# State products of a recursion cut in halves, an addition put behind a negation, an affine step on another engine, and identity products joined

## What is computed

```python
def step(s, inp):                       # the recurrent mixer, per head
    r_t, w_t, k_t, v_t, kk_t, b_t = inp
    sa = jnp.einsum('bhvk,bhk->bhv', s, kk_t)
    s = s * w_t[:, :, None, :] - sa[..., None] * b_t[:, :, None, :] + v_t[..., None] * k_t[:, :, None, :]
    y = jnp.einsum('bhvk,bhk->bhv', s, r_t)
    return s, y
...
z = layer_norm(z, conv_ln_w, conv_ln_b)  # the convolution half
z = z * jax.nn.sigmoid(z)
...
x = x + jnp.concatenate([y_a, y_b], axis=-1) @ w_out
x = x + moe_ffn(h2)                      # top 4 of 32 experts, w_gate, w_up, w_down
```

## Time and profile before

| | us |
|---|---|
| median of 3 runs | 1165.84 (1164.99 to 1166.95) |
| the profiled execution | 1165.45 |
| its span, first to last instruction | 1163.6 |
| PE busy | 1122.2 (96%) |
| DVE busy | 529.1 (45%) |
| ACT busy | 212.3 (18%) |
| bytes moved | 430.00 MB, mean 370 GB/s |

### The profile page before, as it was taken

One profiled execution on the slowest core, in us unless ns is written; L12 is line 12 of the kernel. 1 busy time (PEld: TensorE's weight loads), 2 busy tenths in 40 slices (PEclk: granted clock), 3 DMA queues, 4 the chain that ended last, 5 costly groups with the idle time before them and its releaser, 6 DMA issues.

```text
span 1163.6 us, 16613 instructions
## 1 busy us (share of the span) xinstructions
PE 1122.2 (96%) x6608; PEld 480.4 (41%) x6608; DVE 529.1 (45%) x1123; ACT 212.3 (18%) x433; POOL 34.1 (3%) x47
## 2 busy tenths in 40 slices
PE   9999999999999999999999999999999999999997
PEld 7666786643333333333333333333333333333332
DVE  6999965337333333333333333333333333333333
ACT  3265642221111111111111111111111111110012
POOL 0002412000000000000000000000000000000000
PEclk9999999999999999999999999999999999999999
DMA  9724006999999999999999999999999999999995
GB/s 247 214 86 179 20 16 175 429 392 415 417 427 427 429 428 430 427 429 427 430 429 427 430 427 430 428 429 427 430 427 429 430 426 430 429 429 427 429 421 204
DMA packets 58587, 430.00 MB, mean 370 GB/s; under 512 B 16670, under 2 KB 29390, under 8 KB 34220
## 3 DMA queue, kind: packets, MB, share of 16 engines
q1 hardware_dynamic: 58288, 428.84, 89.7%
q10 hardware_dynamic: 260, 0.61, 0.2%
HBM read 424.92 MB, written 4.48 MB: 369 GB/s over the span
## 4 chain that ended last, share of the span: by engine, by line
PE 53%; DMA 29%; DVE 4%; issue 1%; ACT 1%; DVEq 0%; ACTq 0%
PE bank L2166 35%; DMA ring<-in_w_up_dram 26%; PE bank L2133 5%; DMA arena<-in_w_up_dram 3%; PE bank L2140 2%; PE bank L2086 2%; PE bank L1734 2%; DVE arena L2536 1%; DVE arena L2560 1%; PE bank L1312 1%; PE bank L1271 1%; PE bank L2174 1%; PE bank L2192 1%; PE bank L1320 0%; PE bank L278 0%
## 5 line engine op out<-in xcount | busy, mean ns | idle before, releaser
L2166 PE MATMUL bank<-arena 128*64 128x512 f32 x1540 | 344.2, 594 | 11.4 <-DMA arena<-in_w_up_dram 11.2
L2166 PE MATMUL bank<-ring,arena 128*64 128x512 f32 x1532 | 342.2, 594 | 11.8 <-DMA ring<-in_w_up_dram 11.0
L2166 PEld LDWEIGHTS bank<-arena 128*64 128x64 f32 x1540 | 108.0, 136 | 225.8 <-issue 197.9
L2166 PEld LDWEIGHTS bank<-ring,arena 128*64 128x64 f32 x1532 | 108.0, 137 | 225.2 <-issue 198.0
L2560 DVE TENSOR_TENSOR arena<-arena,bank 128x512 f32<-128x512 f32 x180 | 110.0, 680 | 0.0
L2549 DVE SCALAR_TENSOR_TENSOR arena<-bank,arena 128x512 f32<-128x512 f32 x31 | 23.3, 751 | 182.0 <-ACT arena L1928 182.0
L2536 DVE TENSOR_SCALAR arena<-bank 128x512 f32<-128x512 f32 x31 | 21.4, 692 | 179.9 <-PE bank L2174 179.9
L610 PE MATMUL bank<-arena,ring 128*128 128x336 f32 x352 | 102.5, 447 | 0.3 <-DVE arena L751 0.3
L2133 PE MATMUL bank<-arena 128*64 128x512 f32 x372 | 86.7, 599 | 4.3 <-DVE arena L2560 0.6
L1904 ACT COPY arena<-bank 128x512 f32<-128x512 f32 x31 | 18.2, 587 | 354.3 <-PE bank L2133 354.3
L610 PEld LDWEIGHTS bank<-arena,ring 128*128 128x128 f32 x352 | 65.8, 189 | 34.2 <-issue 2.9
(11 more groups left out here) (387 smaller groups left out, 785.5 us busy)
## 6 DMA issues: line engine op xcount, KB each, us to landing
ring<-in_w_gate_dram SPq DMA_DIRECT2D x32, 2048.0 KB, 29.8
arena<-in_w_up_dram SPq DMA_DIRECT2D x32, 2048.0 KB, 32.8
arena<-in_w_gate_dram SPq DMA_DIRECT2D x32, 2048.0 KB, 29.9
arena<-in_w_down_dram SPq DMA_DIRECT2D x31, 2048.0 KB, 35.4
ring<-in_w_down_dram SPq DMA_DIRECT2D x31, 2048.0 KB, 35.4
ring<-in_w_up_dram SPq DMA_DIRECT2D x29, 2048.0 KB, 32.9
ring<-in_w_in_dram SPq DMA_DIRECT2D x11, 1024.0 KB, 8.4
ring<-in_w_up_dram SPq DMA_DIRECT2D x11, 512.0 KB, 7.3
```

The lines of the kernel that those rows point to most:

```text
L2166: mm = M.matmul(bank[64 * hb:64 * hb + 64, b, :], tokens(cc), rows[:, 512 * hb:512 * hb + 512], start=(cc == 0), stop=(w3 == 2 and cc == K ...
```

## The change

Four edits, all in the scan:
1. `state(j)` is cut into `state(j, 0)` and `state(j, 1)`. The half for r = 0 stays at the end of step j; the half for r = 1 runs in step j + 1, behind W and the identity product and ahead of U. `st_done` is raised by the second half.
2. On DVE the addition to `sout` stands behind the negation of U instead of ahead of it.
3. The affine step of `zT` moves from DVE (one quarter ahead of the loop, one in each of three steps) to ACT: four activations with scale and bias, in place, between the first and second `take_v`.
4. The eight identity products of a step become one product with the whole 128 x 128 identity over 256 columns; the eight products with `identc` in step 0 become two over 256 columns each.

```diff
@@ scan_act
             take_v(0)
+            for j in range(4):
+                nc.scalar.activation(zT[:, j, :], zT[:, j, :], ACT.Identity, bias=vecA[:, V_CLB + j:V_CLB + j + 1],
+                                     scale=vecA[:, V_CLW + j:V_CLW + j + 1]).then_inc(S["z_scaled"], 1)
             take_v(1)
@@ scan_pe
-            def state(j):
...
-                for r in range(2):
-                    for i in range(2):
-                        at = 64 * i + 32 * r
-                        mm = M.matmul(bank[side(r), 6 + i, 0:256], VU[2][at:at + 32, i, 1, j, :],
-                                      KBxx[at:at + 32, j, i], start=True, stop=True)
-                mm.then_inc(S["st_done"], 1)
+            def state(j, r):
+
+                if r == 0:
+                    if j == 0:
+                        pe.wait_ge(S["e_ready"], 4)
+                        pe.wait_ge(S["un5_ready"], 2)
+                    else:
+                        pe.wait_ge(S["sout_ready"], j)
+                for i in range(2):
+                    at = 64 * i + 32 * r
+                    mm = M.matmul(bank[side(r), 6 + i, 0:256], VU[2][at:at + 32, i, 1, j, :],
+                                  KBxx[at:at + 32, j, i], start=True, stop=True)
+                if r == 1:
+                    mm.then_inc(S["st_done"], 1)
@@ the loop
-                    each(4, identity, kept_state, 64, C, True, False)
+                    M.matmul(bank[:, 4, 0:256], ident, Zc.rearrange("p j k -> p (j k)"), start=True, stop=False)
+                    state(c - 1, 1)
@@
                 if c == 0:
-                    each(7, lambda i, j: identc, lambda i, j: szb[:, i, j, 0, :], 64, C, True, False)
+                    for i in range(2):
+                        M.matmul(bank1(7)[side(i)], identc, szb[:, i, :, 0, :], start=True, stop=False)
@@
                 if c < 4:
-                    state(c)
+                    state(c, 0)
@@ scan_dve
-            z_affine(0)
             level(5, 0)
             level(5, 1)
@@ the loop
+                dve.wait_ge(S["u_done"], c + 1)
+                negated(c // 2, c % 2, 2).then_inc(S["un_ready"], 1)
+                if c:
                     dve.wait_ge(S["old_read"], c)
                     dve.wait_ge(S["st_done"], c)
                     kept = sout[:, c - 1, :].rearrange("p (s i k) -> p i s k", s=4, i=2)
                     V.tensor_tensor(kept, bank[:, 6:8, 0:256].rearrange("p i (s k) -> p i s k", s=4), kept, ALU.add)\
                         .then_inc(S["sout_ready"], 1)
-                dve.wait_ge(S["u_done"], c + 1)
-                negated(c // 2, c % 2, 2).then_inc(S["un_ready"], 1)
@@
-                if c < 3:
-                    z_affine(c + 1)
```

More of the change, by code:

```diff
@@ L988, in build @@
         names = ["v_turned", "vtok_ready", "hat_ready",
-                 "last_turned", "last_copied", "z_scaled", "z_sig", "zT_ready",
+                 "last_turned", "last_copied", "z_scaled", "zT_ready",
                  "kb_turned", "kbtok_ready", "sc_done", "sc_read", "blk_done",
@@ L1081, in scan_act @@
                 nc.scalar.activation(zsg[:, j, :], zT[:, j, :], ACT.Sigmoid, bias=vecA[:, V_CLB + j:V_CLB + j + 1],
-                                     scale=vecA[:, V_CLW + j:V_CLW + j + 1]).then_inc(S["z_sig"], 1)
+                                     scale=vecA[:, V_CLW + j:V_CLW + j + 1])
             def take_v(p):
@@ L1331, in rows @@
                 return v[64 * i:64 * i + n]
-            def identity(i, j):
-                return ident[side(i), side(i)]
             def chunk(c):
@@ L1553, in level @@
                                 b2(clow[:, l - 4, :], 8), ALU.mult).then_inc(S["e_ready"], 1)
[L1555 to L1558, removed]
             dve.wait_ge(S["kb_turned"], 6)
```

## The result

The changed kernel takes 1166.84 us (median of 18 runs, 1165.62 to 1169.19), the kernel before 1164.92 us in as many runs beside it (1163.07 to 1166.95). The ratio is 1.0019, with a 95% interval of 1.0013 to 1.0026: the change makes the kernel **2.2 us slower**, 1.5 to 3.0 (the two medians are 1.9 us apart). The forecast was +2.0 us, or +0.17%, and 1167.8 us.

What follows compares the result with a forecast made beforehand. PE's own order bounds the scan, the expert weight stream the back. Steps sum to 0.46 + 0.50 + 0.50 + 0.57 - 0.03 = +2.00 us; 1165.45 + 2.00 + 0.39 gives 1167.8 us, range 1164.5 to 1169.4.

Steps and rivals of the forecast that it cites:

- The bound: Behind the scan, the expert weight stream bounds; a PE shift reaches the end one to one, at least 2.8 us if earlier.
- rival (c): Behind the scan: PE's shift doesn't reach the end, as the stream is set by its start at 196.94; 1165.8 us, chance 0.06.
- A half costs what the whole costs: State products in the scan: a half takes 0.56 us (0.53 to 0.59) against 0.59 for the whole.
- Rival (a): In the scan: halves cost half, shapes nothing extra; -1.05 us, 1164.8 us (best case 1163.9), chance 0.13 with its best case.
- the second rival: What the prediction said a reading by instruction counts alone would give; second in its list stands Rival (b).
- the joined product: Between W and the second half of state: 0.62 us, 0.43 of work and 0.19 for leaving the shape.
- Rival (b): In the scan: each extra change of shape costs 0.25 us, 12 extra blocks, +3.2 us, 1169.1 us, chance 0.18.
- The sum: W to U 1.54 us in place of 1.01; +0.50 in steps 2 and 3, +0.57 in step 4, +2.00 in all.
- the change behind W: Change of tile shape between W and the whole-array identity product: 0.13 us.
- The stall of step 1: W's instructions stall 0.24 us in step 1; if that stays, W to U is 1.78 against 1.29, +0.46 us.
- Cost 0: DVE's addition moved behind the negation: at most 0.03 us gain per step, taken as 0, and no cost.
- The cover of 0.18: On DVE: the moved addition would end about 172.45, 0.18 us ahead of the next evacuation at 172.63.

Runs made afterwards that it cites:

- SP late: The kernel before with one more wait of SP ahead of the first expert weights, which start 5.0 us later: ratio 0.9999 of before (0.9990 to 1.0008).
- PE late: The kernel before with ten extra whole-array products of 336 columns into an unused bank in step 4: ratio 1.0042 of before (1.0028 to 1.0056), 4.9 us longer.

## Why the prediction was right, and where it wasn't

- **The bound.** Right: SP late cost nothing that shows (0.9999), which with the 2.2 us also ends rival (c); PE late and PE earlier (no state products) both moved the end in the size of their shift, within their intervals. One reading was loose: the waits for weights are summed from 230 us on the earlier trace rows, but the first of them comes at 610 us. Up to there PE carries a shift along by itself; only behind it does the place of the stream, which by the windows is set by about 294 us, take over.
- **A half costs what the whole costs.** Right, a little more than said: 0.58 for either half, where 0.56 was taken, and 0.59 for the whole. Rival (a), halves at half the price, is dead: W starts 0.58 after the half, not 0.30. (It is this one, and not the second rival, that a reading by instruction counts gives.)
- **Changes of shape.** W's group took 0.39 with its change where 0.36 was summed, the joined product 0.63 where 0.62 was. Rival (b), 0.25 for each change, didn't come (its sum, 1165.84 + 3.2, is 1169.0 and not 1169.1).
- **The sum.** W to U is 1.60, forecast 1.54; per step +0.58, forecast +0.50. In step 4 +0.59, forecast +0.57. The whole loop is +2.28 without the stall, forecast +2.00. The mis-sized terms are the half (0.02 too small, twice), the change behind W (0.03) and the joined product (0.01).
- **The stall of step 1.** The sum took 0.24 for something that may belong to the step. It doesn't: it was absent in the second trace of before and in both of after, and present in the trace with the late PE and in the one with the products unjoined.
- **Luck in the number.** Trace against trace the loop grew by 25.59 - 23.58 = 2.01, which looks like the forecast to the hundredth. But the terms were 0.28 too small together, and the 0.27 of the stall, which happened to be in this trace of before and not in that of after, hides it. The 1167.8 lies 1.0 above the median measured, mostly because the kernel before had a median of 1164.92 in the runs beside it and not the 1165.84 of its first three.
- **The second edit.** "Cost 0" holds for the change as a whole and for this edit alone, but the reasoning missed its worth: with the halves it saves 0.32 us in each of steps 1 and 2 (4.48 to 4.16), since the halves make the addition late. (Between these two kernels the affine step moved too; the chain shows the addition as what was waited for.) The cover of 0.18 behind it came out as 0.14.
- **The fourth edit.** Beside the halves it costs 0.18 per step in steps 1 to 3 (4.16 to 4.34). The forecast's terms hold 0.13 + 0.62 for it where the eight products took 0.46 and a change behind them, which the prediction puts at 0.16, so 0.13; measured it is 1.60 against 1.42. Alone it gains about 0.2 in the loop by sharing the shape of the projection, which the forecast didn't see.
- **The third edit.** No effect, as said: ACT waited 1.02 behind it where 0.9 was forecast.
- **First weights.** Forecast at 197, seen at 198.42, and at 199.58 in the second trace of the unchanged kernel, so the change isn't needed for it. It was of no consequence, as SP late shows.
- **Behind the loop.** The prediction looked only for transfers in the chain there. That DVE, with POOL beside it, could make PE later by 0.6 us was not in the sum; the last section tells it.

## What to carry to other kernels

Products that sit side by side in different parts of the array took the time of one here (0.59 us for four, 0.58 for two): halving their number halved nothing, and the second half paid in full in its new place. Count the changes of tile shape (0.10 to 0.20 us each in these traces) beside the instructions, and put a product beside one of its own shape. Before work is moved to another step, look for what is queued behind it on the other engines. If two traces are to be compared for where a shift of a few microseconds went, take a second trace of the same kernel first.

## What the runs showed of the hardware that was not expected

**DVE and POOL slow each other.** Behind the loop, in the trace of after, PE waits for DVE for 0.53 us where it didn't before:

```profile
198.01 4.57 DVE L2366 SCALAR_TENSOR_TENSOR arena<-arena 128x336 f32<-128x336 f32 x4
...
204.93 0.85 PE L2017 MATMUL bank<-arena 32*128 32x336 f32 x8 [0.53 <-DVE arena L2370]
```

```profile
196.62 5.60 POOL L1848 TENSOR_TENSOR arena<-arena 128x336 f32<-128x336 f32 x5 [30.71 <-DMA arena<-kept_rows]
```

In the trace of before POOL starts 0.3 us into the same four instructions (L2370 there):

```profile
194.86 3.94 DVE L2370 SCALAR_TENSOR_TENSOR arena<-arena 128x336 f32<-128x336 f32 x4
...
195.16 6.10 POOL L1852 TENSOR_TENSOR arena<-arena 128x336 f32<-128x336 f32 x6 [29.74 <-DMA arena<-kept_rows]
...
198.83 2.25 DVE L2374 RECIPROCAL arena<-arena 128x336 f32<-128x336 f32 x1
```

And in the kernel with only the second and third edit POOL comes behind them:

```profile
195.44 2.01 DVE L2366 SCALAR_TENSOR_TENSOR arena<-arena 128x336 f32<-128x336 f32 x4
...
198.93 6.50 POOL L1848 TENSOR_TENSOR arena<-arena 128x336 f32<-128x336 f32 x7 [32.67 <-DMA arena<-kept_rows]
```

One such instruction takes 0.57 us with POOL idle and 1.20 with POOL adding beside it. The four together take 2.01, 3.94 or 4.57 us as none, three or all of them fall beside POOL (2.65 for one, in the second trace of before). DVE's RECIPROCAL, which reads one tile where the four read two, takes 2.25 us in all three traces (2.26 in after). POOL pays too: five of its additions take 5.60 us in after, while a single one beside the RECIPROCAL takes 0.90 (at 202.68 in the same trace).

POOL starts when SP's transfer of the kept rows lands, PE and DVE when the loop is done, so it is the place of the one against the other that counts. From the end of the loop to the group of products at 587 us, ten of the fourteen traces take 401.22 to 401.27 us. Both traces of after take 401.85 and 401.86, the kernel with only the second and third edit 401.93, the one without state products 402.24. In these last two POOL's additions fall beside a later addition of DVE that PE waits for. The halves alone and the products unjoined, whose loops end 2 us later as well, lose nothing there. So the 0.6 us of after is not a plain result of its late loop; why the kept rows land earlier against DVE in it stays open. In the runs' median this part can't be told apart. That the two engines contend was not tried by an experiment of its own; the rows show the times with and without the overlap.

**Identical code stalls at times.** A gap within the products W of step 1 comes and goes between traces. It makes the step 0.27 us longer in the first trace of before, 0.48 with the products unjoined and 0.56 with PE late. Gaps in other places exist too: 0.24 ahead of the loop in the second trace of after, 0.15 in step 3 with SP late. Their cause stays open.
